# A modulation in four stages instead of two halves, a swapped order in one norm, and last halves one after the other

## The reference

```python
ada = (c @ w_ada + b_ada)[:, None, :]
shift1, scale1, gate1, shift2, scale2, gate2 = jnp.split(ada, 6, axis=-1)
h = rmsnorm(x, g_norm1) * (1.0 + scale1) + shift1
proj = h @ w_in                       # q, k, v, gates, index query and key
...
y = moba_attention(x, a_w_in[j], a_w_out[j], rel_bias)
x = layer_norm(DEEPNORM_ALPHA * x + y, ln_g[i, 1], ln_b[i, 1])
x = layer_norm(DEEPNORM_ALPHA * x + 0.5 * swiglu(x, w_gu, w_down), ln_g[i, 2], ln_b[i, 2])
```

## Time and profile before

| | us |
|---|---|
| median of 3 executions (1347.33 to 1348.98) | 1347.61 |
| the profiled execution, its own time | 1347.83 |
| span from its first to its last instruction | 1346.1 |
| TensorE busy | 1324.5 |
| DVE busy | 876.7 |
| ACT busy | 697.1 |

### The profile page before, as it was taken

The page is one execution under the profiler, slowest core; times in us unless marked ns, Lnnn a source line. Parts: engine busy times, 40 slices in busy tenths (PEclk is TensorE's granted clock), DMA queues, the critical chain, the costliest instruction groups (busy, mean ns, idle before and its releaser), DMA issues.

```text
span 1346.1 us, 17337 instructions
## 1 busy us (share of the span) xinstructions
PE 1324.5 (98%) x6741; PEld 1111.5 (83%) x6741; DVE 876.7 (65%) x1210; ACT 697.1 (52%) x1112; POOL 76.1 (6%) x114
## 2 busy tenths in 40 slices
PE   7999999999999999999999999999999999999997
PEld 5788878888888888888877888888888888888885
DVE  6797768777667665665547664676664676766464
ACT  3765564553545553554665553555554544455452
POOL 1401000000002000001001000001000010100000
PEclk9999999999999999999999999999999999999999
DMA  9967744557455655546517556556655564665641
GB/s 350 319 215 242 278 173 162 182 223 253 181 214 190 191 188 192 196 172 222 188 63 221 186 188 214 192 170 220 208 182 178 185 232 175 206 201 187 199 171 69
DMA packets 160222, 268.45 MB, mean 199 GB/s; under 512 B 9755, under 2 KB 103052, under 8 KB 160012
## 3 DMA queue, kind: packets, MB, share of 16 engines
q1 hardware_dynamic: 152428, 239.47, 52.3%
q0 software_dynamic: 7648, 27.85, 5.9%
q10 hardware_dynamic: 64, 0.02, 0.0%
HBM read 266.21 MB, written 1.07 MB: 199 GB/s over the span
## 4 chain that ended last, share of the span: by engine, by line
PE 94%; DVE 2%; DMA 2%; ACT 1%; issue 0%; SPq 0%; POOL 0%; DVEq 0%; ACTq 0%; POOLq 0%
PE TBB L843 12%; PE UPP L843 12%; PE Y L791 10%; PE Y L792 10%; PE Y L793 10%; PE UPP L791 7%; PE UPP L793 7%; PE UPP L792 7%; PE TBB L844 6%; PE UPP L844 6%; PE TBB L888 2%; DMA WADA<-in_w_ada 1%; PE Y L920 1%; DVE ADA L1851 1%; PE Y L927 1%
## 5 line engine op out<-in xcount | busy, mean ns | idle before, releaser
L1730 DVE TENSOR_TENSOR WL<-RAW,WH 128x1024 fp32r<-128x1024 f32 (+1 forms) x434 | 499.2, 1197 | 170.4 <-ACT WH L1313 166.6
L1313 ACT CAST WH<-RAW 128x1024 fp32r<-128x1024 f32 (+1 forms) x434 | 421.6, 1028 | 195.0 <-PE Y L793 70.4
L843 PE MATMUL UPP<-AHL,WH 128*128 128x512 f32 x672 | 240.2, 400 | 0.0
L843 PE MATMUL TBB<-AHL,WH 128*128 128x512 f32 x672 | 238.8, 398 | 0.0
L791 PE MATMUL Y<-WH,HH 128*128 128x512 f32 (+1 forms) x496 | 192.1, 387 | 0.0
L793 PE MATMUL Y<-WH,HL 128*128 128x512 f32 (+1 forms) x496 | 191.4, 386 | 0.0
L792 PE MATMUL Y<-WL,HH 128*128 128x512 f32 (+1 forms) x496 | 191.3, 386 | 0.0
L844 PE MATMUL TBB<-AHL,WL 128*128 128x256 f32 x672 | 188.4, 280 | 0.0
L844 PE MATMUL UPP<-AHL,WL 128*128 128x256 f32 x672 | 188.4, 280 | 0.0
L791 PE MATMUL UPP<-WH,AHL 128*128 128x512 f32 x432 | 176.8, 409 | 1.0 <-DVE AHL L1736 0.5
L793 PE MATMUL UPP<-WH,AHL 128*128 128x512 f32 x432 | 169.0, 391 | 0.0
(11 more groups left out here) (260 smaller groups left out, 1382.9 us busy)
## 6 DMA issues: line engine op xcount, KB each, us to landing
RAW<-in_ffn_w_gu SPq DMA_DIRECT2D x176, 512.0 KB, 4.9
RAW<-in_ffn_w_down SPq DMA_DIRECT2D x80, 512.0 KB, 4.3
RAW<-in_w_mlp SPq DMA_DIRECT2D x64, 512.0 KB, 4.4
RAW<-in_w_in SPq DMA_DIRECT2D x34, 512.0 KB, 6.1
PIECE<-in_w_ada POOLq DMA_DIRECT2D x32, 512.0 KB, 5.9
RAW<-in_a_w_in SPq DMA_DIRECT2D x24, 512.0 KB, 4.8
WADA<-in_w_ada SPq DMA_DIRECT2D x14, 512.0 KB, 9.3
RAW<-in_w_out SPq DMA_DIRECT2D x8, 512.0 KB, 4.3
```

The lines of the kernel that those rows point to most:

```text
L843: pe.matmul(banks[:, block, :], WH[:, u % 2, w], AHL[:, k, :], start=k == 0, stop=False)
L1313: act.copy(WH[:, u % 2, q * n:(q + 1) * n], raw_half(u, q // 2)[:, (q % 2) * n:(q % 2 + 1) * n]).then_inc(wh_done, 1)
L1730: ve.tensor_tensor(WL[:, u % 2, o], raw_half(u, q // 2)[:, (q % 2) * n:(q % 2 + 1) * n], WH[:, u % 2, o].bitcast(F32), ALU.subtract).then_ ...
```

## The change

`ada_half` is replaced by `ada_quarter`: the modulation comes in four stages of two k-tiles, each with eight pieces of 256 KB (rows of 1 KB). In each stage TensorE makes unit 0's two k-tiles, `ada_first` of the next stage, unit 1's two k-tiles with fp32 products, and `ada_columns` of the next stage. So unit 1's k-tiles 4 and 5 are now fp32 products too and only its last quarter is rounded and split. `ada_first` of the first stage stands behind the transposes, and four constant products are left of twelve. SP loads unit 1 in four parts between the pieces; buffers move (unit 1's second half into Z, unit 3's first half into the room of the old pieces), and waits with them. For "c3" alone, `scaled` of tok 0 comes before the first two quarters of the split, and quarter 0 of unit ("aout", 1) is rounded before the last `my_high` and split before the last `my_low`. In the last unit, tok 1, all products of the first bank come before those of the second, and `begin` can read the first bank when it is done.

```diff
...
@@ -573,19 +574,15 @@
             wada = t["w_ada"].rearrange("(k p) n -> p k n", p=P)[:, :, 0:2 * D].rearrange(
                 "p k (a n) -> p k a n", a=2)
 
-            def ada_half(h):
-
-                for k in range(KT - 1):
-                    if h:
-                        sp.wait_ge(*((wada_read, 1) if k == 0 else (wada_used, k)))
-                    sp.dma_start(WADA[:, k, :, :], wada[:, k, :, h * HALF:(h + 1) * HALF]).then_inc(in_wada[k], 16)
-                if h:
-                    sp.wait_ge(acc_done, 2)
-                for pair in range(2):
-                    s = slice(pair * 2 * P, (pair + 1) * 2 * P)
-                    sp.dma_start(WADA[:, KT - 1, :, s],
-                                 wada[:, KT - 1, :, h * HALF + pair * 2 * P:h * HALF + (pair + 1) * 2 * P]
-                                 ).then_inc((in_wada[KT - 1], in_last)[pair], 16)
+            def ada_quarter(st):
+
+                c = slice((st % 2) * 2 * P, (st % 2 + 1) * 2 * P)
+                for k in range(KT):
+                    if st >= 2:
+                        sp.wait_ge(*((wada_read, st - 1) if k == 0 else (acc_done, st - 1) if k == KT - 1 else
+                                     (wada_used, (KT - 2) * (st - 2) + k)))
+                    sp.dma_start(WADA[:, k, :, c], wada[:, k, :, st * 2 * P:(st + 1) * 2 * P]
+                                 ).then_inc(in_wada[k][st % 2], 16)
 
             def raw_parts(u, half):
 
@@ -629,14 +626,22 @@
 
             for tok in range(TOK):
                 sp.dma_start(X[:, tok, :], t["x"][0, tok * P:(tok + 1) * P, :]).then_inc(in_x[tok], 16)
-            ada_half(0)
+            def first_query(part):
+
+                dd, ss = raw_parts(1, part // 2)[part % 2]
+                sp.dma_start(dd, ss).then_inc(raw1_in[part], 16)
+
+            ada_quarter(0)
             raw_load(0, 0)
-            raw_load(1, 0)
-            ada_half(1)
+            first_query(0)
+            ada_quarter(1)
+            first_query(1)
+            ada_quarter(2)
             raw_load(0, 1)
-            sp.wait_ge(wada_read, 2)
-            sp.wait_ge(wada_used, KT - 1)
-            raw_load(1, 1)
+            sp.wait_ge(tr_done, TURN["h", 1, 1] + 1)
+            first_query(2)
+            ada_quarter(3)
+            first_query(3)
             sp.dma_start(BF[:, :], t["b_forget"].partition_broadcast(P)).then_inc(in_small, 16)
             sp.dma_start(REL[0:NB, :], t["rel_bias"]).then_inc(in_small, 16)
             sp.dma_start(ONEHOT[:, :], t["onehot"]).then_inc(in_small, 16)
...
@@ -858,16 +866,22 @@
                     pe.wait_ge(br_read, 3)
                 elif first and product in DEEP and banks is None:
                     pe.wait_ge(y_free[tok], DEEP[product])
-                for k in ks:
-                    for h in range(2):
-                        if turns and (k, h) == (2, 1):
-                            chain_turns(*turns)
-                        o = k * D + h * HALF
-                        quarters(u, tok, o + HALF)
-                        w = slice(o, o + HALF)
-                        mm = three(dst[h][:, :], ah[:, k0 + k, ts], al[:, k0 + k, ts], WH[:, u % 2, w],
-                                   WL[:, u % 2, w], first and k == 0, last and k == kts - 1)
+                closing = (u, tok) == (len(UNITS) - 1, 1)
+                steps = [(k, h) for k in ks for h in range(2)]
+                if closing:
+                    steps.sort(key=lambda kh: kh[1])
+                for k, h in steps:
+                    if turns and (k, h) == (2, 1):
+                        chain_turns(*turns)
+                    o = k * D + h * HALF
+                    quarters(u, tok, o + HALF)
+                    w = slice(o, o + HALF)
+                    mm = three(dst[h][:, :], ah[:, k0 + k, ts], al[:, k0 + k, ts], WH[:, u % 2, w],
+                               WL[:, u % 2, w], first and k == 0, last and k == kts - 1)
+                    if not closing:
                         quarter_taken(mm, u, tok, o + HALF)
+                    elif (k, h) == (kts - 1, 0):
+                        mm.then_inc(half_done, 1)
                 if ks[-1] == kts - 1:
                     mm.then_inc(mm_done, 1)
 
@@ -968,30 +982,26 @@
                 for _ in range(n):
                     pe.matmul(dst[:, 0:REV], IDR[:, :], CMR[:, :], start=True, stop=True)
 
...
+            def ada_first(st):
+
+                if st >= 2:
+                    pe.wait_ge(scale_done, st - 1)
+                pe.matmul(Y[0][st % 2][:, 0:4], ONES[0:64, :], IDENT[0:64, 64:68], start=True, stop=False)
+                pe.wait_ge(in_wada[0][st % 2], 16 * (st // 2 + 1))
                 for a in range(2):
                     for k in range(2):
...
+                        o = (st % 2) * 2 * P + k * P
+                        mm = pe.matmul(Y[0][st % 2][:, 2 * a + k:2 * a + k + 1], WADA[:, 0, a, o:o + P], CC[:, 0:1],
+                                       start=False, stop=False)
+                mm.then_inc(wada_read, 1)
+
+            def ada_columns(st):
+
+                pe.wait_ge(acc_done, st + 1)
+                for a in range(2):
+                    for k in range(2):
+                        c = 2 * st + k
+                        mm = pe.matmul(Y[0][st % 2][:, 2 * a + k:2 * a + k + 1], ADA[:, a, c * P:(c + 1) * P],
                                        ONES[:, 0:1], start=False, stop=a == 1 and k == 1)
                 mm.then_inc(ada_done, 1)
 
...
@@ -1025,35 +1037,27 @@
                             mm.then_inc(mm_done, 1)
 
             pe.wait_ge(*emptied(TURN[("col",)]))
-            ada_begin(0)
-            for pair in range(2):
-                for a in range(2):
-                    ada_first(pair, a)
             for tok in range(TOK):
                 pe.wait_ge(xhat_done, tok + 1)
                 chain_turns("h", tok, Z)
-            constant_products(12, UP[0])
-            for pair in range(2):
-                ada_columns(0, pair)
-            for k in range(4):
-                for tok in range(TOK):
-                    opening_raw(0, tok, k)
-            ada_begin(1)
-            for k in range(4):
-                for tok in range(TOK):
-                    opening_raw(1, tok, k)
-                    if k < 2:
-                        ada_first(k, tok)
-            ada_columns(1, 0)
-            ada_columns(1, 1)
-            for k in range(4, KT):
-                for tok in range(TOK):
-                    opening_raw(0, tok, k)
+            constant_products(4, UP[0])
+            ada_first(0)
+            ada_columns(0)
+            for st in range(4):
+                for k in (2 * st, 2 * st + 1):
+                    for tok in range(TOK):
+                        opening_raw(0, tok, k)
+                if st < 3:
+                    ada_first(st + 1)
+                    for k in (2 * st, 2 * st + 1):
+                        for tok in range(TOK):
+                            opening_raw(1, tok, k)
+                    ada_columns(st + 1)
             pe.wait_ge(in_small, 48)
             rev_row(0)
-            opening(1, (0,), range(4, KT))
+            opening(1, (0,), range(6, KT))
             from_tmp(("qi", 0), 3)
-            opening(1, (1,), range(4, KT))
+            opening(1, (1,), range(6, KT))
             from_tmp(("qi", 1), 3)
             from_tmp(("qf", 0), 4)
 
...
@@ -1441,7 +1445,7 @@
             mod_highs(1)
             mod_highs(2)
             mod_highs(3)
-            round_unit(1, (2, 3))
+            round_unit(1, (3,))
             taken(("tab", 0), REVROW[:, :], REV)
 
             for tok in range(TOK):
@@ -1671,9 +1675,10 @@
                 if att == 2 * NF + 5:
                     my_high(1, 0)
                 att += 1
+            round_unit(UNIT[("aout", 1)], (0,))
             for tok in range(TOK):
                 my_high(tok, 1)
-            round_unit(UNIT[("aout", 1)])
+            round_unit(UNIT[("aout", 1)], (1, 2, 3))
             norm_high("c3", UNIT[("aout", 1)] + 1, False)
             ffn(1, "c3")
             norm_high(("f", 1), UNIT[("dn", 1, 5)] + 1, False)
@@ -1817,8 +1822,11 @@
                 signal = tmp_v if turned else out_ready
                 begin(0)
                 centre(0, rms, gain)
-                split_unit(u, (0, 1))
+                if name != "c3":
+                    split_unit(u, (0, 1))
                 scaled(name, 0, rms, dst, offset, signal)
+                if name == "c3":
+                    split_unit(u, (0, 1))
                 split_unit(u, (2, 3))
                 if turned:
                     chain_low(name, 0)
@@ -1840,26 +1848,21 @@
             ve.wait_ge(*emptied(TURN[("col",)]))
             step(ve.tensor_scalar(COLS[:, 8:16], COLS[:, 8:16], 1.0, None, ALU.add))
 
-            def ada_sums(h):
-
-                acc = ADA[:, 0:2, h * HALF:(h + 1) * HALF]
-                for k in range(1, KT - 1):
-                    ve.wait_ge(in_wada[k], 16 * (h + 1))
```

(54 more changed lines are left out.)

55 lines of the change are left out of this document (22 added, 33 removed).

## The result

| | before | changed |
|---|---|---|
| median (number of executions), us | 1347.47 (4) | 1359.63 (4) |
| lowest and highest, us | 1347.02, 1348.98 | 1356.52, 1361.36 |
| profiled execution, its own time, us | 1347.83 | 1356.52 |
| its span, us | 1346.1 | 1354.8 |

The ratio is 1.0086, with a 95% interval of 1.0069 to 1.0103: the changed kernel is slower by 12.2 us, where I had forecast 4.4 us. The direction was right; the size wasn't, and 1359.63 lies above my range. A second set of four executions gave 1357.37 (1355.09 to 1360.67; further down). So the changed kernel also scatters over 5 to 6 us, the kernel before over 2 us in the same comparison.

The account below looks back on a forecast made before the run. TensorE, busy for 98% of the span, was taken to bound the kernel. Opening +4.3, third norm +0.7 and end -0.6 summed to +4.4 us, 1352.0 us on the median, with a range of 1348.8 to 1357.5.

Parts of the forecast that it names:

- The opening's chain: Opening: each stage is a chain on TensorE of 9.1 us, so unit 0 ends 4.3 us later than now.
- three waits of about 1.1: Opening, a sign: TensorE waits three times about 1.1 us for the modulation on DVE before unit 0's last product.
- The transfers: Opening: 32 smaller pieces take about 2.1 us more; by transfers alone unit 0 ends at 43.7, 1.7 us behind now.
- The last piece: Opening, a sign: the last piece of `w_ada` lands near 38.5 us.
- rival 2: Opening: transfers bind, not TensorE; +1.7, with third norm -1.2 and end -0.6 the time is 1347.5; chance 0.13.
- The advice of the Trainium skill on large transfers: Rule against the change: transfers of 1 MiB and more advised; 32 pieces of 256 KB would cost more than 2.1 us.
- ACT's wait: Opening, near 50 us: TensorE waits about 3.4 us for ACT's query copy instead of 0.53.
- unit 1's twelve products fewer: Opening: twelve fp32r products removed, some 2.8 us, lie beside ACT's chain of 42.81 to 49.67 and yield nothing.
- Third norm: Scaling before the splits and the early quarter: next unit starts near 722.0 instead of 721.27, +0.7 us (-1.2 to +1.5).
- End: Last unit's halves one after the other: one of two DVE steps is left, -0.6 us.
- rival 1: TensorE at its low clock in the first stage and the wait near 50: +2 to +4, 1354 to 1356; chance 0.23.
- both places of the opening: Low clock in the first stage (+1.8 and +2.3) and at the 3.4 us wait near 50 (at worst 3 to 4).

Follow-up runs that it names:

- the second fill: The changed kernel with ten constant products in TensorE's wait before the unit behind the third norm: 1357.97 us; together with the first fill 1355.34 us.
- the first fill: The changed kernel with eighteen constant products in TensorE's wait for ACT's query copy: 1356.24 us (1352.53 to 1360.52).

## Why the prediction was wrong

**The opening's chain was right.** First product forecast 16.5, measured 16.83; stage 9.1, measured 9.08; three waits of about 1.1, measured 0.96 each (1.06 the first); unit 0's end 46.1 to 46.3, measured 48.20, and 46.51 without the slow products of the first stage: 4.54 against my 4.3. The products moved out of the third stage took 1.62 off the fourth's start, and DVE was last then, at 7.46 against my 7.0 to 7.4: the bounds that I had given the stage hold as well.

**The transfers were right as the one that isn't last.** The last issues and landings of the pieces of `w_ada` in the changed kernel, between 30 and 41 us (first and last start of an issue; shortest, median and longest time to landing):

```profile
L584 SPq DMA_DIRECT2D WADA<-in_w_ada x4: 467/468/847, 29.8 to 31.7; - x4
...
DMA to landing us min/median/max: 7.3/7.5/7.8
```

The last piece, issued at 31.7, landed by 39.5 (38.5 forecast), and TensorE didn't wait for it: its stage started at 36.69 and the next `ada_columns` at 43.86. SP's issues cost nothing. With that rival 2 falls. The advice of the Trainium skill on large transfers (page "DMA: Bandwidth & Descriptors", section "Bandwidth"), that I had weighed and set aside, had no bearing on the time here.

**ACT's wait** was forecast as 3.4 and is 3.26; unit 1's twelve products fewer brought nothing, as said.

**Third norm.** The wait was right: TensorE waits 1.88 (about 2 forecast). I had summed it to +0.7 at the unit behind it, and there it is 0.0 in the traces that have both edits. What I had left out is what the splits in one piece do to the next weights: they come free later, and inside the unit 0.6 to 1.15 are lost in the six profiles of kernels with both edits whose clock stayed up (0.6 in the norm's edits alone, 0.8 with the second fill, with or without the first). So the size of the term came out, at another place and by a path that I hadn't named: that is luck.

**End.** -0.6 forecast, -0.6 in the chain.

**What failed is rival 1, TensorE at its low clock.** I had both places of the opening, named the right rows, and gave it 2 to 4 us and a chance of 0.23, with nothing of it in the forecast. The step that failed is the 0 us that the sum has for it: the profiled execution lost 1.69 + 2.49 = 4.2 us to it in the opening, about what the chain itself cost (4.5). Three things in my treatment were wrong. First, I took it as a case that may or may not happen. In all eleven profiles of a kernel with the four-stage opening, unit 0's first eight products run at the low level in whole or in part, and take 3.6 to 4.8 instead of 2.5; in two it lasted to 31 us. Of the six profiles of the two-half opening, two have unit 0's first sixteen at 6.42 instead of 4.73. Behind the 3.26 us wait it came in four profiles of five, behind the 1.9 us wait of the norm in five of seven. Second, I missed the third place: I forecast a wait of 2 us in front of the unit behind the norm and priced only the wait. 1.6 us follow it, of which 0.4 to 1.0 are the clock's, as 0.6 to 1.15 are lost there without it. Third, my typical price of 2 to 4 us was too low for both places of the opening together, 4.2 with a short low stretch at the front; the long one of the kernel with the first fill ended unit 0 another 5.96 later.

The sum for the profiled execution was missed by 4.3 (8.7 against 4.4): 0.2 in the chain, 4.2 by the clock in the opening, 0.9 more at the norm, 0.1 in between, and 1.06 back from the stretch behind 744 us, which I had no term for. Without that last piece of luck it would be 9.8. The median lies 3.1 above this execution. A longer low stretch at the front is the likely reason, but no execution of the first set except the lowest has a trace, so it isn't shown.

The earlier trace rows had a hint: the changed opening has a pause of 1 us in each 9 and sparse work around it, where TensorE in the kernel before is busy almost without a gap for 14 us. It isn't the whole reason, since the three later stages have the same pause and run at the full level, and filling the first pause didn't bring the first stage to it. Why the first stage falls stays open.

The Trainium skill, page "TensorE: Matmul & The Clock Gate", section "HAM oscillation — how this bites in real kernels", tells of a kernel whose products start at the low clock after each wait. I had cited it and set it aside with "no row here shows a pause like it". That was true of the rows before and no argument: the pauses were those that I had forecast myself. The runs agree with the section's pattern in part: behind the 3.26 us wait the products started low in four profiles of five, at 2.49 us in the changed kernel's; behind the three waits of 0.96 in its trace they didn't.

**Without the clock** the change costs a little more than I forecast, as far as the runs can tell. The lowest executions of four-stage kernels that keep the products in their place took 1352.53 and 1352.69, with mean clocks of 0.997 and 0.999: 4.7 and 5.2 over the medians of the kernel before beside them, against 4.4. These are the lowest of four each, so this is an indication, not a measurement. The trace with both late waits filled gives the same order: its span is 8.2 over the kernel before's, of which 1.69 are the slow first stage and 1.08 the stretch between 930 and 990 us; 5.4 are left.

What stays open is what decides, from one execution to the next, how long the front stays low: neither constants at the start nor a fill in the pause settled it.

## What to carry to other kernels

Before you cut a stage of dense work into smaller ones, list each pause of TensorE that the new order makes, the small ones too, and price behind each the next few microseconds of products at twice their length; on this kernel two low stretches in the opening cost 4.2 us, about as much as the chain that made them, and one behind the norm at most 1 more. If such a price is likely it belongs into the forecast's sum, not into a rival. And when a fill seems to cure it, run it again: kernels whose executions lie 5 to 8 us apart can't be told from one another by four of them, while a trace can show for one execution which place fell. Follow the delay past the place that you filled, too: behind the norm the clock's loss had covered a wait for DVE that came out when the clock stayed up.

## What I hadn't expected of the hardware

The granted clock of the profile leaves out the low stretch at the very start: 1.00 stood beside products of 6.60 us that take 3.68. The durations of equal instructions are the safer sign there.

Waits alike didn't act alike: behind the same 3.26 us wait the clock fell in one execution and not in another. The two-half opening fell in three profiles of six, once behind 1.83 us and twice at unit 0's first products, in one of these with no wait longer than 0.17 us in front of them.

TensorE has two gaits in the attention's split products, at the same full clock. Its timeline in the kernel before, and then in the changed kernel, at the same instructions:

```profile
758.07 0.40 PE L843 MATMUL UPP<-AHL,WH 128*128 128x512 f32 x1
...
758.78 0.40 PE L843 MATMUL UPP<-AHL,WH 128*128 128x512 f32 x1
```

```profile
767.89 0.39 PE L851 MATMUL UPP<-AHL,WH 128*128 128x512 f32 x1
...
768.58 0.39 PE L851 MATMUL UPP<-AHL,WH 128*128 128x512 f32 x1
```

Two pairs of products take 0.71 us in the one and 0.69 in the other, 2% over some 58 us: this is the 1.06 that came back between 744 and 803. The order alone in the norm shows the same there. A like stretch lies between 930 and 990 us, where the norm's edits alone and three kernels with fills lost 1.08. All five profiles with the low level behind the norm have the faster gait from 744 on, but so have three of the twelve others, so the low level isn't needed for it. No run was made for it and its cause stays open; it is one more source of differences of 1 us that no edit aimed at.
